# Hybrid decoder trunk on one core: query stage of the latent attention reordered, its norm weight applied at the evacuation

## The reference, cut to what matters

```python
def mla_queries(cq, pos, q_a_g, w_q_b, q_norm_g):
    q = jnp.einsum('btr,rhe->bthe', rmsnorm(cq, q_a_g), w_q_b)
    q = jnp.concatenate([q[..., :MLA_NOPE], rope(q[..., MLA_NOPE:], pos)], axis=-1)
    return rmsnorm(q, q_norm_g)

def mla_keys(ckv, kpe, w_kb, k_norm_g):
    kn = jnp.einsum('blr,rhe->blhe', ckv, w_kb)
    kp = jnp.broadcast_to(kpe[:, :, None, :], kn.shape[:-1] + (MLA_ROPE,)).astype(kn.dtype)
    return rmsnorm(jnp.concatenate([kn, kp], axis=-1), k_norm_g)
```

## Time and profile before

| | us |
|---|---|
| runs | 3013.89, 3017.01, 3020.87 |
| median | 3017.01 |
| profiled execution | 3020.83 |
| its span | 3019.0 |
| query stage, layer 1 and 2 | 75.67, 76.02 |
| prompt stage, layer 1 and 2 | 38.88, 38.80 |

### The profile page before, as it was taken

One profiled execution on the slowest core, in us unless ns is written; L12 is line 12 of the kernel. 1 busy time (PEld: TensorE's weight loads), 2 busy tenths in 40 slices (PEclk: granted clock), 3 DMA queues, 4 the chain that ended last, 5 costly groups with the idle time before them and its releaser, 6 DMA issues. The chain is left out here.

```text
span 3019.0 us, 62226 instructions
## 1 busy us (share of the span) xinstructions
PE 2689.8 (89%) x24160; PEld 2464.3 (82%) x24160; DVE 1898.7 (63%) x3163; ACT 1353.0 (45%) x2302; POOL 843.6 (28%) x696
## 2 busy tenths in 40 slices
PE   7986878999988889899988877699999898998998
PEld 6876457999988689899877763499999795898998
DVE  4844456777766655489358453567777676554993
ACT  4733344555544343354366334345555442433542
POOL 0030006999930400000000300079999204000000
PEclk9999988999998999999989989799999999998999
DMA  5324329967545375465453233298776354763654
GB/s 133 105 64 120 97 57 147 155 110 135 87 81 157 87 203 162 110 162 140 117 126 88 76 105 108 56 165 140 128 116 93 65 158 117 189 165 101 165 138 120
DMA packets 832231, 365.86 MB, mean 121 GB/s; under 512 B 400045, under 2 KB 819414, under 8 KB 831368
## 3 DMA queue, kind: packets, MB, share of 16 engines
q1 hardware_dynamic: 829714, 360.77, 52.4%
q10 hardware_dynamic: 2232, 1.26, 0.2%
HBM read 342.63 MB, written 61.23 MB: 134 GB/s over the span
## 5 line engine op out<-in xcount | busy, mean ns | idle before, releaser
L1170 PE MATMUL key_banks<-w_kb_head,latent_T_head 128*128 128x352 f32 x1536 | 519.8, 338 | 29.3 <-DVE latent_T_rest L1317 25.8
L1170 PE MATMUL key_banks<-w_kb_rest,latent_T_head 128*128 128x352 f32 x1536 | 496.4, 323 | 0.0
L1170 PE MATMUL key_banks<-w_kb_head,latent_T_rest 128*128 128x352 f32 x1536 | 495.6, 323 | 0.0
L293 DVE TENSOR_TENSOR w_rests<-w_ring,w_heads 128x2048 fp32r<-128x2048 f32 (+1 forms) x152 | 326.2, 2150 | 165.4 <-ACT w_heads L287 165.2
L1170 PEld LDWEIGHTS key_banks<-w_kb_head,latent_T_head 128*128 128x128 f32 x1536 | 290.9, 189 | 43.3 <-issue 27.5
L1331 DVE TENSOR_REDUCE w_kb<-key_sq 128x8 f32<-128x1024 f32 x256 | 310.7, 1214 | 11.9 <-ACT key_sq L1243 7.7
L952 POOL TENSOR_TENSOR rwkv_state_tmp<-rwkv_state,vec 128x1024 f32<-128x1024 f32 x64 | 154.4, 2413 | 538.8 <-DMA rwkv_state<-in_state_rwkv_dram 534.0
L287 ACT CAST w_heads<-w_ring 128x2048 fp32r<-128x2048 f32 (+1 forms) x152 | 272.6, 1796 | 54.6 <-ACT conv_last_rows L1873 19.7
L1170 PEld LDWEIGHTS key_banks<-w_kb_rest,latent_T_head 128*128 128x128 f32 x1536 | 291.3, 190 | 0.0
L1170 PEld LDWEIGHTS key_banks<-w_kb_head,latent_T_rest 128*128 128x128 f32 x1536 | 290.1, 189 | 0.0
L1230 ACT CAST latent_T_head<-turn_bank 128x256 fp32r<-128x256 f32 x256 | 95.6, 373 | 409.9 <-PE key_banks L1174 380.3
(11 more groups left out here) (567 smaller groups left out, 7033.3 us busy)
## 6 DMA issues: line engine op xcount, KB each, us to landing
w_ring<-in_ffn_w_up_dram SPq DMA_DIRECT2D x88, 512.0 KB, 5.0
page_latents<-in_cache_kv_latent_dram SPq DMA_DIRECT2D x256, 128.0 KB, 2.4
latent_blocks<-page_latents SPq DMA_DIRECT2D x256, 128.0 KB, 3.8
latents<-page_latents SPq DMA_DIRECT2D x64, 512.0 KB, 8.3
w_ring<-in_w_in_dram SPq DMA_DIRECT2D x52, 512.0 KB, 3.8
w_ring<-in_w_gate_dram SPq DMA_DIRECT2D x48, 512.0 KB, 4.0
w_ring<-in_w_in_dram SPq DMA_DIRECT2D x20, 1024.0 KB, 6.4
w_ring<-in_ffn_w_down_dram SPq DMA_DIRECT2D x32, 384.0 KB, 3.2
```

What stands on the lines that cost most here:

```text
L293: ops.tensor_tensor(rests[:, slot, 0:tiles * P], ring[:, slot, 0:tiles * P], heads[:, slot, 0:tiles * P].bitcast(F32), ALU.subtract).then_ ...
L1170: last = nc.tensor.matmul(kbank[:, 3 * x + n, 0:KB], c[:, x, r * P:(r + 1) * P], w[:, r, cols], start=r == 0 and m == 0, stop=r == 1 and m ...
```

## The change

In the query stage TensorE first makes keys and values of both prompt tiles, then queries of all three tiles, each into three banks on end, and then turns tile 0 and tile 1 only. ScalarE copies a tile's queries with one instruction. Squares and sums of keys are made before the queries stand. The product of both norm weights is turned to the partitions (two turns, two small copies to `gain_T`), and multiplied in as the scale of the evacuation of the turned queries, instead of by VectorE on the rows. The order of the groups is all of q, then all of k.

Sample queries are only copied and rotated there (by VectorE, into `sam_q`, a part of the squares' buffer that now outlives the stage). Their norm runs in the prompt stage: Square, Ln and Exp at the head of ScalarE's program, the sum at the head of VectorE's, the product after head 1's norm, the 16 turns after step 4 of TensorE, their evacuation with the weight in step 5 of ScalarE.

The RWKV sample rows are no longer turned by TensorE: one VectorE transposition in blocks of 32 by 32 turns all 1536 columns at the head of its program. The rows then lie on four groups of 32 partitions, with 32 floats on end; SP stores them with four DMAs ahead of its gathers.

Of the pages gathered, 10 go to `mla_project` (after the loads of `w_kb` and `w_vb`), 25 stay in `mla_qkv`, 10 in `mla_prompt`, and 39 are left to `cache_attention`.

```diff
-GATHER = {"tiles": range(0, 44), "qkv": range(44, 76), "prompt": range(76, 88), "cache": range(88, NB * PAGES)}
+GATHER = {"tiles": range(0, 44), "project": range(44, 54), "qkv": range(54, 79), "prompt": range(79, 89), "cache": range(89, NB * PAGES)}
@@ mla_project, sync
                     sp.dma_start(buf[:, :, :], k.ldram(name).rearrange("(t p) h e -> p t (h e)", p=P)).then_inc(kv_in, 16)
+                copied = gather_pages(sp, k, GATHER["project"], gathered)
...
+                sp.wait_ge(gathered, copied)
@@ mla_qkv
+        Q_BANKS = ((4, 5, 6), (0, 1, 2), (3, 4, 5))
+        GROUPS = [(what, part, half) for what in ("q", "k") for half in range(2) for part in range(2)]
...
-                products(0)
-                products(1)
-                turns(0)
-                products(2)
-                turns(1)
-                turns(2)
+                keys_values(0)
+                pe.wait_ge(gain_made, 1)
+                nc.tensor.transpose(banks[:, 7, 0:32], gain[0:32, 0:NOPE], k.col("ident", 0, 32, 32))
+                nc.tensor.transpose(banks[0:ROPE, 7, 32:64], gain[0:32, NOPE:QK], k.col("ident", 0, 32, 32)).then_inc(gain_turned, 1)
+                keys_values(1)
+                pe.wait_ge(loaded, 16)
+                queries(0)
+                pe.wait_ge(k_kept, 2)
+                pe.wait_ge(v_kept, 2)
+                queries(1)
+                pe.wait_ge(q_kept, 1)
+                queries(2)
+                pe.wait_ge(gain_kept, 1)
+                turns(0)
+                turns(1)
@@ scalar
+                def norm_queries(n):
+                    act.wait_ge(q_made, n + 1)
+                    nc.scalar.copy(q_tm[:, n, :, :].rearrange("p h e -> p (h e)"), q_in_banks(n).rearrange("p a b -> p (a b)")).then_inc(q_kept, 1)
                     act.wait_ge(q_rope, n + 1)
...
+                    nc.scalar.activation(sq[:, 0, :, :], q_tm[:, n, :, :], ACT.Square).then_inc(q_squared, 1)
...
+                            nc.scalar.activation(dst, src, ACT.Copy, scale=k.gain_T[0:r, part:part + 1]).then_inc(t_kept, 1)
...
+                keep_keys_values(0)
+                keep_keys_values(1)
+                norm_queries(0)
+                act.wait_ge(gain_kept, 1)
+                norm_queries(1)
                 turned_out(0)
                 turned_out(1)
@@ vector
+                keys(0)
+                keys(1)
...
+                queries(0)
+                queries(1)
+                dve.wait_ge(q_made, 3)
+                c(nc.vector.tensor_copy(k.sam_q.rearrange("p h e -> p (h e)"), q_in_banks(2).rearrange("p a b -> p (a b)")))
+                rotate(k.sam_q, rot[0:NSAM, :, :, :], 2)
@@ mla_prompt
-        rows = st.sb("sample_rows", [NSAM, 6, D])
+        rows = st.sb("sample_rows", [P, 6, DT, 32])
+        SAM_AT = 4
@@ sync
+                sp.wait_ge(row_turned, 1)
+                out_rows = k.vec_rows.rearrange("n (t x) r (y f) -> x y r (n t) f", x=2, y=2)
+                for q in range(4):
+                    sp.dma_start(out_rows[q // 2, q % 2], rows[32 * q:32 * q + 32, :, :, :].rearrange("r n t f -> r (n t) f")).then_inc(rows_out, 16)
                 copied = gather_pages(sp, k, GATHER["prompt"], gathered)
-                sp.wait_ge(row_kept, 12)
-                for n in range(6):
-                    sp.dma_start(k.vec_rows[n].rearrange("h r d -> r h d"),
-                                 rows[:, n, :].rearrange("r (h d) -> r h d", d=64)).then_inc(rows_out, 16)
@@ tensor
-                    if h < HEADS:
-                        row_turns(h)
...
+                    if h == SAM_AT:
+                        pe.wait_ge(sam_normed, 1)
+                        for part, e in enumerate((slice(0, NOPE), slice(NOPE, QK))):
+                            r = (NOPE, ROPE)[part]
+                            for head in range(HEADS):
+                                last = nc.tensor.transpose(banks[0:r, 6 + part, head * NSAM:(head + 1) * NSAM], k.sam_q[:, head, e],
+                                                           k.col("ident", 0, NSAM, NSAM))
+                            last.then_inc(sam_turned, 1)
@@ scalar
+                nc.scalar.activation(k.sam_sq, k.sam_q, ACT.Square).then_inc(sam_squared, 1)
+                act.wait_ge(sam_summed, 1)
+                nc.scalar.activation(sam_ss[:, :], sam_ss[:, :], ACT.Ln, bias=k.col("eps", rows=NSAM), scale=1.0 / QK).then_inc(sam_inverse, 1)
...
+                    if h == SAM_AT + 1:
+                        for part, dst in enumerate((k.qnT, k.qrT)):
...
@@ vector
+                nc.vector.transpose(rows[:, :, :, :].rearrange("p n t f -> p (n t f)"),
+                                    k.samT[:, :, :, :].rearrange("p n t r -> p (n t r)")).then_inc(row_turned, 1)
+                dve.wait_ge(sam_squared, 1)
+                nc.vector.tensor_reduce(sam_ss[:, :], k.sam_sq, AX.X, ALU.add).then_inc(sam_summed, 1)
...
-                        for g in row_groups(h):
-                            dve.wait_ge(row_turned, g + 1)
-                            nc.vector.tensor_copy(rows[:, g // 2, g % 2 * 512:(g % 2 + 1) * 512], banks[0:NSAM, 6 + g % 2, :]).then_inc(row_kept, 1)
+                    if h == 2:
+                        dve.wait_ge(sam_inverse, 2)
+                        nc.vector.tensor_tensor(k.sam_q, k.sam_q, bc(sam_ss[:, :], QK), ALU.mult).then_inc(sam_normed, 1)
```

More of the change, by code:

```diff
@@ L578, in _, with keys_values, queries @@
             def _(pe):
-                def products(n):
+                def keys_values(n):
                     first, rows = TOK[n]
[L581 to L596, removed]
+                    for b0, w, kept in ((0, k.w_kb, k_kept), (2, k.w_vb, v_kept)):
+                        if n:
+                            pe.wait_ge(kept, n)
+                        for j in range(2):
+                            for t in range(2):
+                                last = nc.tensor.matmul(banks[:, b0 + j, :], k.ckvT[:, t, first:first + rows], w[:, t, j * 512:(j + 1) * 512],
+                                                        start=t == 0, stop=t == 1)
+                        last.then_inc(kv_made, 1)
+                def queries(n):
+                    first, rows = TOK[n]
+                    for j, b in enumerate(Q_BANKS[n]):
                         for t in range(4):
@@ L599, in products @@
                                                     start=t == 0, stop=t == 3)
-                    last.then_inc(made, 1)
+                    last.then_inc(q_made, 1)
                 def turns(n):
[L603 to L607, removed]
+                    for g, (what, part, half) in enumerate(GROUPS):
+                        if g == 0:
+                            pe.wait_ge(q_normed, n + 1)
+                        if g == 4:
+                            pe.wait_ge(k_normed, n + 1)
+                        if 8 * n + g >= 2:
+                            pe.wait_ge(t_kept, 8 * n + g - 1)
                         src = q_tm if what == "q" else k_tm
@@ L617, in _ @@
+                pe.wait_ge(k_kept, 2)
[4 more added lines that the diff above has]
+                pe.wait_ge(gain_kept, 1)
                 turns(0)
-                products(2)
                 turns(1)
-                turns(2)
             @block.scalar
             def _(act):
[L624 to L637, removed]
-                    nc.scalar.copy(flat[:, 1024:1536], banks[0:rows, 0, :]).then_inc(q_kept, 1)
@@ L697, in _ @@
-                    last.then_inc(summed, 1)
-                    dve.wait_ge(inverse, 2 * n + 2)
-                    c(nc.vector.tensor_tensor(q, q, bc(ss[0:rows, 0, :], QK), ALU.mult))
-                    last = nc.vector.tensor_tensor(q, q, gain[0:rows, :].unsqueeze(1).to_broadcast([rows, HEADS, QK]), ALU.mult)
-                    if n < 2:
-                        last = nc.vector.tensor_tensor(k_tm[:, x, :, :], k_tm[:, x, :, :], bc(ss[:, 1, :], QK), ALU.mult)
-                    last.then_inc(normed, 1)
+                    return nc.vector.tensor_tensor(x2, r[:, 2, :, :], r[:, 3, :, :], ALU.add)
```

122 lines of the change are left out of this document (64 added, 58 removed).

## The result

The changed kernel takes 2994.59 us (median of 4 runs, 2991.43 to 2999.6), the kernel before beside it 3018.94: ratio 0.9908, 95% interval 0.9888 to 0.9928. It is faster, by 24.4 us. The forecast was 2971 with a range of 2960 to 2990, so more than 40% of the forecast gain is missing and the time lies outside the range. The profiled execution went from a span of 3019.0 us to 2991.5, so 27.5 us of the 46.3 came.

What follows compares the result with a forecast made beforehand. Compute was taken to bound both stages, SP close behind. Savings of 16.8 + 6.2 us in layer 1 and 17.1 + 6.2 in layer 2, 46.3 us, from 3017.0 gave 2970.7, forecast as 2971; range 2960 to 2990.

Steps and rivals of the forecast that it cites:

- the last reason of the prompt stage: Prompt-stage opening: VectorE's added transposition and reduce, ready at 3.4 us, cost nothing, since scores came at 3.8 us before.
- its 9.27 us pause: Query stage before the change: TensorE's largest wait, ahead of the last turns, for VectorE's gain product of the sample queries.
- the 8.5 kept: Prompt-stage tail: time from score 7's end to the next stage, 8.5 us, taken unchanged from the kernel before.
- the 6.2 us forecast: Prompt stage: predicted saving per layer, ending at 32.4 to 33 us instead of 38.88.
- the 2.25 and 9.27 us waits: Query stage before the change: TensorE's waits ahead of the second tile's turns and the last turns, predicted gone.
- I cost it at nothing: Query-stage evacuation of turned queries: the scaled copy replaces one copy, so no added time was counted.
- The tie of ScalarE and TensorE: Query stage, first turns: ScalarE predicted free at 372.0, TensorE at 372.5, so neither would wait long.
- rival (b): SP becomes the bound through many short stores: prompt stage 3 us longer, whole at 2978; chance 0.12.
- (a): Clock falls at the query stage's turns and first prompt scores: 2 to 6.5 us a layer, 2981; chance 0.22.
- (c): Kernel slower than before through the prompt stage's 128-byte stores into DRAM; 3032 at 100 ns a run; chance 0.03.
- (d): SP or a barrier takes the gain back, as by stalled gathers: 10 to 25 us a layer, 3011 to 3017; chance 0.04.
- everything outside the two stages the same to 1 us: Predicted sign for the rest of the kernel: stages other than query and prompt keep their times within 1 us.

Runs made afterwards that it cites:

- e7: Kernel before the change, with nine unread matmuls in TensorE's 9.3 us pause ahead of the last query-stage turns and one behind them: 3027.05 us, ratio 0.9988.
- e6: Changed kernel with one ScalarE wait dropped and the sample-query products placed between the turns of tile 0 and tile 1: 2998.82 us, ratio 0.9895.
- e3: Changed kernel with the RWKV sample rows turned by TensorE and copied by VectorE again, stored by six DMAs behind the gathers: 3004.3 us, ratio 0.9925.
- e8: Changed kernel with one ScalarE wait, unread matmuls among and behind the query-stage turns, and two in the prompt stage's opening: 2986.9 us, ratio 0.9854.
- e13: Changed kernel with one ScalarE wait and two unread matmuls in the prompt stage's opening, none ahead of the barrier: 2989.02 us, ratio 0.9867.
- e9: e8 with the sample rows turned by TensorE and copied by VectorE again, stored by six DMAs behind the gathers: 3003.18 us, ratio 0.9907.
- e12: Kernel before the change, with thirteen unread matmuls in the 9.3 us pause, one behind the turns and two in the prompt opening: 3033.7 us, ratio 1.0004.
- e2: Changed kernel without ScalarE's wait for the key sums ahead of Ln, keeping only the wait for the query sums: 3000.85 us, ratio 0.9894.
- e11: e8 with turned queries and keys evacuated by a plain copy, leaving out the norm weight of the prompt's queries: 2991.84 us, ratio 0.9865.
- e4: Changed kernel with the page gathers back in place: none in the projection stage, 32 in the query stage, 12 in the prompt stage: 3023.33 us, ratio 0.9973.
- e0: The changed kernel unaltered, run again beside other follow-ups: 3002.26 us, ratio 0.9903.
- e5: Changed kernel with one ScalarE wait and unread matmuls among and behind the query-stage turns, none in the prompt opening: 2981.8 us, ratio 0.9832.
- e1: Changed kernel with an unread matmul after every second group of query-stage turns and one behind the last: 2987.74 us, ratio 0.9858.

## Why the prediction was wrong

**The step that failed** is the last reason of the prompt stage: "In the kernel before they came 3.8 us after the start, with TensorE at the low clock after its 9.27 us pause". The forecast put the low clock down to the pause and so took it to be gone with it. In the kernel before it did come with the pause (fall at 393.9), and filling the pause does hold the clock as long as it is filled (e7: 1.00 from 392.6 to 406.3). But the barrier and the scores of the first heads, thin work with 0.8 to 1.4 us of nothing ahead, mostly bring one by themselves (e7, e6 in spite of dense products between the turns; not in e3's layer 2), and dense work there prevented it in each of the 12 stages traced (e8 to e13). After the change it came 2 us into the stage and lasted 20.5 us, where in the kernel before it came 7 us ahead of the stage and took 9.8 us of it and 3.4 of its tail (mean clock 0.83 in the earlier trace rows; now 0.73). Its price is 38.18 - 31.56 = 6.6 us a layer, 13.2 in all.

**The work of the prompt stage was sized nearly right.** At 1.00 it takes 31.6 us (forecast 32.4 to 33) and 3.15 us a head (forecast 2.99 to 3.0). That the sum came so near has some luck in it: heads and waits took more, and the tail less, 7.2 us from the end of the last scores instead of the 8.5 kept, of which 3.4 had been at the low clock. The transposition took 1.78 us (forecast 1.7, bounds 1.5 and 2.5), the reduce behind it 1.70 (1.75), the sixteen turns 0.94 (1.0), the product 1.74. But what the change saves there is less than it seemed: with the clock held in both, 34.95 - 31.56 = 3.4 us. The rows give 6.8 (e9 against e8), and the sample queries' norm and turns, with the new order of the row turns around them, take 3.5 back (38.40 - 34.95, e9 against e12; no run has them alone). So of the 6.2 us forecast, nearly half, 2.8, were the clock's return and not work.

**Query stage, 2.6 us a layer short.** Turns, order and ends were as forecast, and the 2.25 and 9.27 us waits are gone. The stage began 1.85 us later than before; by that shift the forecast had the products through at 374.35, the first evacuation at about 374.9 and the next stage at 386.25. They came at 375.2, 377.1 and 388.80. The terms: 0.8 us from the first eight products (6.23 us against 5.41 in the earlier trace rows: the low clock with which the stage begins lasted 5.2 us into it and not 3.5); 1.35 us of ScalarE behind two waits (e2), which the forecast missed by taking VectorE's idle of 1.90 us for Ln and Exp (it is 3.25 now, since this step waits for two sums); 0.4 us for "I cost it at nothing" (e11). The tie of ScalarE and TensorE at the first turns became a pause of 1.49 us. With the one wait and the clock up, e13 takes 59.1 us against the 58.9 forecast.

**The gathers were right**: ten in the projection stage end at 314.4 with SP's next issue at 323.3, the twenty-five landed 4.8 us ahead of TensorE (2 forecast, with a stage 2.6 us shorter), and e4 gave the gain of 3.9 us with all 32 left in place, against 4. The stores were not: 3.97 us to issue and 5.2 until the first gather, against 2.6. In the kernel after, the low clock hides it (SP waits 7.7 us at the end); in e8 SP waits 0.7 us for TensorE and in e13 0.2 and 1.3 in the two layers, where the forecast had 5. So rival (b) is next in line, by the stores' extra 2.6 us and not by the gathers.

**The rivals.** (a), the clock falls, was the case, but in another place: a pair of groups cost 1.31 to 1.52 us at 1.00, and the whole price is in the prompt stage. It was given 2 to 6.5 us a layer, "I say 2981", chance 0.22; measured 6.6, and with the query stage's terms the range's end at 2990 didn't hold it. It priced the scores of two heads at half speed; the spell reached to head 5's. Of the Trainium skill's page "TensorE: Matmul & The Clock Gate", section "Part 4: PE-mode transpose", by which the full clock doesn't engage for transposes, the traces show the contrary for these turns: 12 us of them at 1.00 throughout in the kernel after, and in e3's layer 2 the clock came back from 0.50 while TensorE did nothing else. Among turns it did fall, for 3.4 us, in six stages (e3 and e4 in one layer, e7 and e12 in both). (c) and (d) didn't come. But "everything outside the two stages the same to 1 us" didn't hold either: from TensorE's first product in the projection stage to the query stage it was 47.1 us before and 50.7 after in layer 1, and 48.6 and 48.4 in layer 2. The ten gathers are not shown to be the reason: e4, without them there, has 49.0, and e0, with them, 47.4.

**The best version** is the changed kernel with one wait on ScalarE and unread products around the barrier: e5 at 0.9832 [0.9807, 0.9857] and e8 at 0.9854 [0.9828, 0.9880], which can't be told apart, against 0.9903 [0.9866, 0.9941] and 0.9908 for the changed kernel. Open is why e1, with nothing in the opening, held the clock in both layers and e5 in one only, why e3 held it in one with nothing unread at all, and how thin the opening may be; two stages a profile don't settle it.

## What to carry to other kernels

A low clock in a profile has a cause that is to be tested before its return is counted as a gain: look at every thin stretch ahead of the fall, barriers and the first products of a stage among them, not only at the longest pause. Where TensorE is the bound behind a barrier, two matmuls that nobody reads, in the stage's opening, are worth a try: with 1.5 us of their own in it the stage was 6.5 us shorter than the changed kernel's and 3.4 shorter than e2's, whose spell was the shorter one (e13). And a table load of ScalarE goes as early as the waits in front of its function allow: leave one.

## What the runs showed of the hardware

Once down in the prompt stage the clock stayed at 0.50 for 13.7 or 20.5 us in the longer spells, though TensorE's timeline of the kernel after shows no wait from 388.80 to 421. e2 changes nothing in the prompt stage and moved it by 3.1 us, because its spell was 13.7 us long and not 20.5: a small saving can be given or taken there. A copy with a scale for each partition takes ScalarE 0.69 us for 512 columns of PSUM, a plain one 0.58. The clock can fall and come back within a row of turns (e3, layer 2: 0.50 from 1867.5 to 1870.9, in turns from 1863.1 to 1876.1). Ln and Exp one after the other took a table load of 1.28 us each, in every tile. Four stores of 1536 runs of 128 bytes took SP 3.97 us to issue, six of 512 runs of 256 bytes 3.36 and in e9 3.96.
